# Building a Toeplitz bias matrix by two DMAs through a skewed DRAM scratch instead of a Hankel load and matmuls with a flipped identity

## The chip, the cores and the metric

The kernel runs on one core of a Trainium2 chip. The metric is the device time of one execution in microseconds (us): the median of three runs is 929.63 us (929.59 to 930.97). All data is float32; TensorE multiplies it in split form, as a high part plus a low part.

## What is computed

One layer of a hybrid encoder runs for two groups that share the weights: a prompt of 512 tokens and a sample of 32 new tokens with a cache of 512 keys and values. So there are T = 544 token columns, a model width of 1024, 8 attention heads of 64 and 4 retention heads of 128. What the change touches is the relative-position bias of the attention:

```python
def chunk_attention_prompt(q, k, v, table):          # table: (8, 257)
    ...
    dist = jnp.arange(CHUNK)[:, None] - r[None, :] + ATT_WINDOW
    bias = table[:, jnp.clip(dist, -REL_CLIP, REL_CLIP) + REL_CLIP].astype(jnp.float32)
    ...
    s = jnp.where(valid[None, :, None, None, :], s + bias[None, None], -jnp.inf)
    p = jax.nn.softmax(s, axis=-1).astype(v.dtype)

z   = rms_norm(x) @ w_in                             # 1024 x 5632, all branches
mix = (sigmoid(ga) * (A @ w_attn_out) + sigmoid(gb) * (R @ w_ret_out)) @ w_o
x   = x + rms_norm(mix)
x   = x + rms_norm(relu(rms_norm(x) @ w_ff_up)^2 @ w_ff_down)
```

The bias of a query and a key depends on their distance alone, so for each head it is a Toeplitz matrix: constant along its diagonals. Beyond a distance of 128 it is one value, and a constant added to a whole row falls out of the softmax, so the kernel stores bias minus this far value, for 128 queries by 256 nearest keys and 8 heads: a tile of 128 x 8 x 256, 1 MB.

## The kernel before

Activations lie transposed (features on partitions, 544 tokens along the row). Every projection is cut into column tiles of 128 outputs, grouped by four; "group g, tile j" is column_tile(g, j). A tile is 96 matmul instructions of 272 columns: 8 slices of the contraction, 2 halves of the tokens, and the three products high x high, high x low and low x high. Weights stream in by SyncE's DMA queue, half a megabyte per transfer, into w_raw, which has two halves (buffers) for two tiles each. For each tile ScalarE makes the high part w_hi (split_hi, L493), VectorE the low part w_lo (split_lo, L1116), and TensorE waits for the low part (L776) before the tile. VectorE takes each finished tile from PSUM to z (to_z, L1126).

The order on each engine is written out by hand, and engines meet by semaphores:

- SyncE loads x (five transfers), the first 128 columns of w_in (w_first), the next 128 columns, the cached keys k_cache (1 MB, L363), then the second buffer of w_raw in two transfers (L351, L352). Later loads wait until a buffer's low parts are made.
- TensorE transposes x, runs tiles (0,0) and (0,1), waits for k_cache and transposes it, then runs tiles (0,2) and (0,3) and groups 1 and 2. Tile (0,2) needs both transfers of the second buffer, through L493 and L1116.
- GpSimd prepares the bias table at the start (L396 to L405). It loads the 8 x 257 table, fills each row up to 384 with its last value, stores the 8 rows of 1536 B in DRAM (table_ext, 12 KB), waits until that has landed, and loads a Hankel matrix from it: partition p of head h gets 256 values from place 1 + p on. The rows overlap in DRAM; the load moves 1 MB.
- After group 2 TensorE waits for the Hankel tile and turns it into the Toeplitz form: 16 calls (8 heads by 2 blocks of 128) of a matmul with the flipped identity, which the profile shows as 32 matmuls (L856). They go to the PSUM tile wk. VectorE then subtracts the far value (L1186, from PSUM and hankel into bias), masks a block (L1189) and raises bias_ready.
- The attention loop follows, one pass for two heads. TensorE runs tile (3,0), then waits for pair_ready, bias_ready and attT_ready (L918 to L920) and transposes keys and values. VectorE, behind the bias, copies k_pair and v_pair (L1112), makes low parts, takes tile (3,0) and copies the transposed keys to k_nat (L1254, L1255). TensorE runs tile (3,1) and waits for k_nat before the scores.

ScalarE issues the DMAs of the identity, the gains, the ones and the flipped identity (L501 to L504) ahead of its first work. GpSimd has nothing else to do until the attention ends.

Of the kernel before, what the change touches and what calls it, by code (L numbers as in the profile page):

```python
# [1 line left out]

# [4 lines left out]
D = 1024  # L35
P = 128
KT = D // P
SEQ, DEC = 512, 32
T = SEQ + DEC
# [3 lines left out]
AH, AD = 8, 64  # L43
# [4 lines left out]
TABLE = 2 * CLIP + 1  # L48
# [6 lines left out]
Z_AQ, Z_AK, Z_AV, Z_GATE, Z_SPARE, Z_RQ, Z_RK, Z_RV, Z_RG, Z_SLOTS = 0, 4, 8, 4, 12, 20, 24, 28, 32, 36  # L55


def shape_constants():

    f = np.float32  # L60
    ident = np.eye(P, dtype=f)
    flip = np.ascontiguousarray(ident[::-1])
    half = RD // 2
    inv = (f(10000.0) ** (-np.arange(half, dtype=f) / f(half))).astype(f)
    pos = np.concatenate([np.arange(SEQ), PAST + np.arange(DEC)]).astype(f)
    ang = (inv[:, None] * pos[None, :]).astype(f)
    cos = np.cos(ang.astype(np.float64)).astype(f)
    sin = np.sin(ang.astype(np.float64)).astype(f)
    rope = np.zeros((P, 2, T), f)
    rope[:half, 0] = rope[half:, 0] = cos  # L70

    rope[half:, 1] = -sin
    rope[:half, 1] = sin
    decay = np.zeros((P, RH, RC), f)
    t = np.arange(P)
    for h in range(RH):
        lg = np.log1p(-np.exp2(-5.0 - h))

        key = RD ** -0.5
        decay[:, h, :P] = np.where(t[None, :] >= t[:, None], key * np.exp(-(t[:, None] + 1.0) * lg), 0.0)  # L80
        decay[:, h, P] = np.exp((t + 1.0) * lg)
        decay[:, h, P + 1] = key * np.exp((P - 1.0 - t) * lg)
        decay[:DEC, h, P + 2] = key * np.exp((DEC - 1.0 - t[:DEC]) * lg)
        decay[:, h, P + 3] = np.exp(P * lg)
        decay[:, h, P + 4] = np.exp(DEC * lg)
    return {"ident": ident, "flip": flip, "ones": np.ones((P, P), f), "rope": rope, "decay": decay}


class Order:
# [23 lines left out]
def build(nc, a, outs):  # L113
    fp, fr = mybir.dt.float32, mybir.dt.float32r
    ALU, ACT, AX = mybir.AluOpType, mybir.ActivationFunctionType, mybir.AxisListType
    ctx = ExitStack()

    with ctx:
        def sem(name):
            return ctx.enter_context(nc.semaphore(name))  # L120
# [7 lines left out]
        def place(name, shape, dtype=fp, at=None):  # L128

            size = 4 * int(np.prod(shape[1:]))  # L130
            size += -size % 32
            where = top[0] if at is None else at
            if at is None:
                top[0] += size
                assert top[0] <= first + arena_bytes, (name, top[0] - first - arena_bytes)
            ends[name] = where + size
            return nc.alloc_sbuf_tensor_at(name, shape, dtype, offset=where)

        ends = {}
# [8 lines left out]
        ident = place("ident_sb", [P, P])  # L148
        ones = place("ones_sb", [P, P])
# [4 lines left out]
        rope = place("rope_sb", [P, 2, T])  # L154
        decay = place("decay_sb", [P, RH, RC])
# [8 lines left out]
        z_at = top[0]  # L164
# [9 lines left out]
        y_out = place("y_out", [P, 5, D], at=z_at + 4 * T * Z_RQ)  # L174

        x_nat = place("x_nat", [P, 5, D], at=z_at)
        hankel = place("hankel", [P, AH, 2 * P], at=z_at + 4 * T * Z_RQ)
        k_cache = place("k_cache", [P, 4, AH * AD], at=ends["hankel"])
        table_row = place("table_row", [AH, 3 * P], at=ends["k_cache"])
        flip = place("flip_sb", [P, P], at=ends["table_row"])  # L180
        x_waste = place("x_waste", [P, 2, D], at=ends["flip_sb"])
        assert ends["x_nat"] <= z_at + 4 * T * Z_SPARE and ends["x_waste"] <= work_at

        bias = place("bias", [P, AH, 2 * P], at=z_at + 4 * T * Z_SPARE)
# [50 lines left out]
        wk = ctx.enter_context(nc.psum_tensor("wk", [P, 2048], fp))  # L235
        wk_halves = [wk[:, 1024 * i:1024 * i + 1024].rearrange("p (n c) -> p n c", n=2) for i in range(2)]

        table_ext = nc.dram_tensor("table_ext", (AH, 3 * P), fp, kind="Internal").ap()


        ident_in, const_in = sem("ident_in"), sem("const_in")
        x_in = [sem(f"x_in{t}") for t in range(5)]
        w_first, w_in_sem = sem("w_first"), [sem("w_loaded0"), sem("w_loaded1")]
        cache_k_in, table_in, table_filled, table_out, hankel_in = (
            sem("cache_k_in"), sem("table_in"), sem("table_filled"), sem("table_out"), sem("hankel_in"))
        gains_in, x_tr, x_copied_act, x_copied_dve = sem("gains_in"), sem("x_tr"), sem("x_copied_act"), sem("x_copied_dve")
        x_hi, x_lo, x_sum_act, var_clear = sem("x_hi"), sem("x_lo"), sem("x_sum_act"), sem("var_clear")
        kc_tr, kc_ready, bias_mm, bias_ready = sem("kc_tr"), sem("kc_ready"), sem("bias_mm"), sem("bias_ready")
        sum_mm, var_ready, std_ready, tok_rstd_ready, spread_mm, rstd_ready = (
            sem("sum_mm"), sem("var_ready"), sem("std_ready"), sem("tok_rstd_ready"), sem("spread_mm"), sem("rstd_ready"))  # L250
        hi_ready, lo_ready, mm_done, acc_free = sem("hi_ready"), sem("lo_ready"), sem("mm_done"), sem("acc_free")
# [37 lines left out]
        def halves(ap):  # L289
            return ap.rearrange("p (n c) -> p n c", n=2)  # L290
# [103 lines left out]
        def _(pool):  # L394
            order = Order(pool, pool_order)
            pool.dma_start(table_row[:, 0:TABLE], a["rel_bias_table"]).then_inc(table_in, 16)  # L396

            pool.wait_ge(table_in, 16)
            pool.tensor_copy(table_row[:, TABLE:3 * P],
                             table_row[:, TABLE - 1:TABLE].to_broadcast([AH, 3 * P - TABLE])).then_inc(table_filled, 1)  # L400
            pool.wait_ge(table_filled, 1)
            pool.dma_start(table_ext, table_row[:]).then_inc(table_out, 16)

            pool.wait_ge(table_out, 16)
            pool.dma_start(hankel[:], bass.AP(table_ext.tensor, 1, [[1, P], [3 * P, AH], [1, 2 * P]])).then_inc(hankel_in, 16)  # L405

            pool.wait_ge(scores_mm, 2 * PAIRS)
            pool.dma_start(rope[:], a["rope"]).then_inc(ret_const_in, 16)  # L408
# [79 lines left out]
        def _(act):  # L488
# [12 lines left out]
            act.dma_start(ident[:], a["ident"]).then_inc(ident_in, 16)  # L501
            act.dma_start(gains[:], a["gains"]).then_inc(gains_in, 16)
            act.dma_start(ones[:], a["ones"]).then_inc(const_in, 16)
            act.dma_start(flip[:], a["flip"]).then_inc(const_in, 16)  # L504
            for counter, n in CREDITS.items():
                act.sem_inc(counter, n)
            act.preload_act_table(ACT.Sqrt)
# [252 lines left out]
        def _(pe):  # L760
            def products(dst, whi, wlo, k, hi, lo, start, stop):

                for w, h, begin, end in ((whi, hi, start, False), (whi, lo, False, False), (wlo, hi, False, stop)):
                    for n in range(2):
                        ins = pe.matmul(dst[:, n, 0:HALF], w[:, k, :], h[:, k, HALF * n:HALF * n + HALF], start=begin, stop=end)  # L765
                return ins
# [20 lines left out]
            def tr(out, in_):  # L787
                n = in_.shape[0]
                return pe.transpose(out, in_, ident[0:n, 0:n])  # L789
# [3 lines left out]
            for t, (s, n) in enumerate(TILES):  # L793
# [5 lines left out]
                for k in range(KT):  # L799
                    ins = tr(ps[:, k, :], x_nat[0:n, t, P * k:P * k + P])  # L800
# [37 lines left out]
            for p in range(PAIRS):  # L838
                for t in range(4):
                    ins = tr(wk[:, 512 * p + P * t:512 * p + P * t + P], k_cache[:, t, P * p:P * p + P])  # L840
# [6 lines left out]

            pe.wait_ge(hankel_in, 16)  # L850
            pe.wait_ge(const_in, 32)

            pe.wait_ge(kc_ready, 1)
            for h in range(AH):
                for b in range(2):
                    ins = pe.matmul(wk[:, 256 * h + P * b:256 * h + P * b + P], hankel[:, h, P * (1 - b):P * (1 - b) + P], flip[:],  # L856
                                    start=True, stop=True)
            ins.then_inc(bias_mm, 1)


            def scores(i, e):
# [52 lines left out]
            with pe.Fori(0, PAIRS) as i:  # L914
# [35 lines left out]
                for t, (s, n) in enumerate(TILES):  # L950
                    ins = tr(wk[:, s:s + n], att_nat[0:n, t, :])
# [3 lines left out]
            with pe.Fori(0, RH) as i:  # L955
# [16 lines left out]
                for t, (s, n) in enumerate(TILES):  # L972
                    ins = pe.matmul(wk[:, 1024 + RD * t:1024 + RD * t + RD], rk_nat[0:n, t, :], rv_nat[0:n, t, :], start=True, stop=True)  # L973
# [4 lines left out]
                for t, (s, n) in enumerate(TILES):  # L978
                    out = wk[0:n, RD * t:RD * t + RD]
                    alone = t == 0  # L980
                    ins = pe.matmul(out, ret_a[0:n, s:s + n], rv_nat[0:n, t, :], start=True, stop=alone)  # L981
                    if t == 4:
                        ins = pe.matmul(out, rq[:, s:s + n], state_in[:, bass.ds(i, 1), :].rearrange("p a c -> p (a c)"), start=False, stop=True)
                    elif t:
                        ins = pe.matmul(out, rq[:, s:s + n], states[:, t - 1, :], start=False, stop=True)
                ins.then_inc(ret_o_mm, 1)
                column_tile(g, 3, act_hi, act_lo, half_used=h_half_used)
                for t, (s, n) in enumerate(TILES):
# [3 lines left out]
                    ins = tr(wk[:, 1024 + s:1024 + s + n], ret_n[0:n, t, :])  # L992
# [23 lines left out]
            for k in range(KT):  # L1016
                pe.wait_ge(h2_lo, k + 1)
                for j in range(2):
# [3 lines left out]
                    ins = products(acc[j], w_hi[:, j], w_lo[:, j], k, act_hi, act_lo, k == 0, k == KT - 1)  # L1022
# [4 lines left out]
            for k in range(KT):  # L1027
                if k == 3:
                    spread(2)
                ins = products(wk_halves[1], w_hi_third, w_lo_third, k, act_hi, act_lo, k == 0, k == KT - 1)  # L1030
# [32 lines left out]
            for part, (s, n) in enumerate(PARTS):  # L1063
                for j in range(2):
                    if part == 0:
                        pe.wait_ge(lo_ready, 4 * (G_FFN + 15) + 3 + j)
                    for k in range(KT):
# [7 lines left out]
                        ins = pe.matmul(dst, w_lo[:, j, k, :], mid_hi[:, k, s:s + n], start=False, stop=(k == KT - 1))  # L1075
# [31 lines left out]
        def _(dve):  # L1107
            order = Order(dve, dve_order)
# [71 lines left out]
            with dve.Fori(0, G_RET) as g:  # L1180
                for j in range(4):
                    to_z(g, j, 4 * g + j)
                    split_ahead(g, j)

            dve.wait_ge(bias_mm, 1)
            order.after(dve.tensor_tensor(bias[:], wk[:].rearrange("p (h c) -> p h c", h=AH),  # L1186
                                          hankel[:, :, 2 * P - 1:2 * P].to_broadcast([P, AH, 2 * P]), ALU.subtract))

            dve.memset(bias[0:AD, :, P + AD:2 * P], NEG).then_inc(bias_ready, 1)  # L1189
            order.flatten()  # L1190
# [172 lines left out]
            with dve.Fori(0, 2) as i:  # L1363
                for j in range(4):
# [5 lines left out]
                    ins = dve.tensor_tensor(halves(part_b[:]), wk_halves[j % 2][:, :, 0:HALF],  # L1370
                                            z[:, bass.ds(Z_GATE + KT + m, 1), :].rearrange("p a (n c) -> p (a n) c", n=2), ALU.mult)
# [163 lines left out]
```

## Time and profile before

| | us |
|---|---|
| median of three runs | 929.63 (929.59 to 930.97) |
| span of the profiled execution | 929.0 |
| TensorE matmul busy | 886.9 (95%) |
| TensorE weight load busy | 867.7 (93%) |
| VectorE busy | 476.3 (51%) |
| ScalarE busy | 315.9 (34%) |
| GpSimd busy | 99.0 (11%) |

The profile is one execution: all its times start at the first instruction, and durations are those of this execution. The trace has a chain of waits (the work that ended last, followed back), a timeline for each engine, sums by stretch of time with TensorE's granted clock and the share of time in which the 16 DMA engines were busy, and for the DMA queues the packets, the megabytes and the share of the 16 engines' time that these packets took. That share can be over 100%, where packets overlap. Queue q1 is SyncE's, q10 ScalarE's and q0 GpSimd's.

### The profile page before, as it was taken

Reading aid. Unit: us, or ns where it says so; the run is one execution under the profiler, and the core shown is the slowest. Engines: PE = TensorE matmul, PEld = TensorE weight load, DVE = VectorE, ACT = ScalarE, POOL = GpSimd, SP = SyncE. Lnnn points to the kernel's source line nnn. Section 1 sums busy time; section 2 is a strip of 40 time slices with the busy share of each in tenths; the row PEclk is TensorE's granted clock in tenths of the full one; section 3 lists DMA queues with packets and bytes.
Section 4 is the critical chain, followed back from the end, with each engine's and each line's share of the span. In section 5 each row is a group of like instructions: output and inputs, shape, how many; then the busy total and the mean of one; then the engine's idle time right before and its main releaser. Section 6 shows DMA issues by size and latency. Waiting matters only on the chain.

```text
span 929.0 us, 17032 instructions
## 1 busy us (share of the span) xinstructions
PE 886.9 (95%) x6908; PEld 867.7 (93%) x6908; DVE 476.3 (51%) x735; ACT 315.9 (34%) x457; POOL 99.0 (11%) x71
## 2 busy tenths in 40 slices
PE   7999999999988989899998799999999999999997
PEld 6999999999977978889997699999999999999996
DVE  6233766666758467476534844334433443344326
ACT  6212544445323132245423333113311332133322
POOL 1000000000123031120221700000000000000132
PEclk9999999999988989999998799999999999999997
DMA  9323232122321112112222022222222222222202
GB/s 294 101 78 99 70 102 69 56 69 80 112 78 45 51 45 96 51 46 91 90 91 90 1 83 91 73 80 88 88 91 90 90 90 90 90 92 90 91 1 96
DMA packets 78449, 77.18 MB, mean 83 GB/s; under 512 B 2944, under 2 KB 76304, under 8 KB 78416
## 3 DMA queue, kind: packets, MB, share of 16 engines
q1 hardware_dynamic: 69328, 70.53, 23.1%
q10 hardware_dynamic: 8448, 4.02, 1.6%
q0 software_dynamic: 640, 2.17, 0.7%
q8 instruction: 24, 0.39, 0.2%
q14 instruction: 9, 0.07, 0.0%
HBM read 71.70 MB, written 4.99 MB: 83 GB/s over the span
## 4 chain that ended last, share of the span: by engine, by line
PE 89%; DVE 7%; issue 2%; ACT 1%; POOL 1%; DMA 0%; DVEq 0%; ACTq 0%
PE acc L765 73%; PE wk L789 4%; PE wk L765 3%; PE wk L903 3%; DVE rope_k L1292 2%; DVE scaled L1399 1%; DVE act_lo L1419 1%; PE wk L865 1%; PE wk L864 1%; DVE rk L1293 1%; POOL act_lo L433 1%; PE wk L973 1%; PE wk L822 1%; PE acc L789 1%; PE wk L981 1%
## 5 line engine op out<-in xcount | busy, mean ns | idle before, releaser
L493 ACT ACTIVATE w_hi<-w_raw 128x1024 fp32r<-128x1024 f32 x123 | 130.4, 1060 | 469.3 <-PE acc L765 455.2
L765 PE MATMUL acc<-act_hi,w_hi 128*128 128x272 f32 x1264 | 270.8, 296 | 11.8 <-DVE act_lo L1419 8.6
L765 PE MATMUL acc<-act_hi,w_lo 128*128 128x272 f32 x1264 | 265.2, 292 | 0.0
L765 PE MATMUL acc<-act_lo,w_hi 128*128 128x272 f32 x1264 | 264.6, 291 | 0.0
L765 PEld LDWEIGHTS acc<-act_hi,w_hi 128*128 128x128 f32 x1264 | 202.6, 192 | 17.6 <-DVE act_lo L1419 9.8
L765 PEld LDWEIGHTS acc<-act_lo,w_hi 128*128 128x128 f32 x1264 | 202.5, 192 | 0.0
L765 PEld LDWEIGHTS acc<-act_hi,w_lo 128*128 128x128 f32 x1264 | 201.2, 192 | 0.0
L1116 DVE TENSOR_TENSOR w_lo<-w_raw,w_hi 128x1024 fp32r<-128x1024 f32 x123 | 150.3, 1222 | 35.0 <-ACT w_hi L493 34.9
L765 PE MATMUL acc<-mid_hi,w_hi 128*128 128x272 f32 x608 | 125.4, 287 | 0.0
L765 PE MATMUL acc<-mid_hi,w_lo 128*128 128x272 f32 x608 | 125.0, 288 | 0.0
L765 PE MATMUL acc<-mid_lo,w_hi 128*128 128x272 f32 x608 | 124.8, 287 | 0.0
L765 PEld LDWEIGHTS acc<-mid_lo,w_hi 128*128 128x128 f32 x608 | 95.0, 188 | 0.0
L765 PEld LDWEIGHTS acc<-mid_hi,w_lo 128*128 128x128 f32 x608 | 94.7, 188 | 0.0
L765 PEld LDWEIGHTS acc<-mid_hi,w_hi 128*128 128x128 f32 x608 | 94.7, 188 | 0.0
L1126 DVE TENSOR_TENSOR z<-acc,rstd 128x544 f32 (+1 forms) x44 | 31.8, 722 | 97.9 <-PE acc L765 97.6
L1458 DVE TENSOR_TENSOR y_ffn<-y_ffn,acc 128x544 f32 (+1 forms) x30 | 21.6, 721 | 107.9 <-PE acc L765 107.9
L439 POOL TENSOR_TENSOR sqsum<-sqsum,sq 128x544 f32<-128x544 f32 x20 | 34.4, 1720 | 379.5 <-ACT sq L728 353.4
L1436 DVE SCALAR_TENSOR_TENSOR relu<-acc,rstd 128x544 f32<-128x544 f32 x31 | 22.4, 724 | 81.5 <-PE acc L765 81.4
L562 ACT ACTIVATE probs<-wk,neg_max 128x512 f32<-128x512 f32 (+4 forms) x40 | 22.2, 558 | 16.9 <-DVE neg_max L1215 16.8
L1441 DVE TENSOR_TENSOR mid_lo<-relu,mid_hi 128x544 f32 (+1 forms) x32 | 23.2, 725 | 7.6 <-ACT mid_hi L706 7.5
L408 POOL DMA_DIRECT2D rope_sb<-in_rope x1 | 0.6, 550 | 224.8 <-PE wk L865 224.8
L424 POOL TENSOR_TENSOR rope_q<-rq,rope_sb 64x544 f32<-64x544 f32 x8 | 12.3, 1537 | 93.7 <-DVE rq L1112 93.3
(206 smaller groups left out, 881.6 us busy)
## 6 DMA issues: line engine op xcount, KB each, us to landing
w_raw<-in_w_in SPq DMA_DIRECT2D x44, 512.0 KB, 4.3
w_raw<-in_w_ff_up SPq DMA_DIRECT2D x32, 512.0 KB, 4.3
w_raw<-in_w_ff_down SPq DMA_DIRECT2D x32, 512.0 KB, 4.1
w_raw<-in_w_o SPq DMA_DIRECT2D x8, 512.0 KB, 3.9
x_nat<-in_x_prompt SPq DMA_DIRECT2D x4, 512.0 KB, 5.2
w_raw<-in_w_attn_out SPq DMA_DIRECT2D x4, 512.0 KB, 3.5
w_raw<-in_w_ret_out SPq DMA_DIRECT2D x4, 512.0 KB, 4.5
k_cache<-in_cache_attn_k SPq DMA_DIRECT2D x1, 1024.0 KB, 11.8
```

Source lines behind the costliest of these rows:

```text
L439: pool.tensor_tensor(sqsum[:], sqsum[:], sq[:, m % 2, :], ALU.add).then_inc(sq_added, 1)
L493: act.activation(w_hi[:, v % 2], w_raw[:, v // 2, :, P * (v % 2):P * (v % 2) + P], ACT.Copy).then_inc(hi_ready, 1)
L562: act.activation(probs[0:n, P_COL[t]:P_COL[t] + WIDTH[t]], wk[0:n, S_COL[t]:S_COL[t] + WIDTH[t]], ACT.Exp, bias=neg_max[0:n, t:t + 1], acc ...
L765: ins = pe.matmul(dst[:, n, 0:HALF], w[:, k, :], h[:, k, HALF * n:HALF * n + HALF], start=begin, stop=end)
L789: return pe.transpose(out, in_, ident[0:n, 0:n])
L903: ins = pe.matmul(out, probsT[:, PT_COL[t] + n * b:PT_COL[t] + n * b + n], v, start=(b == 0), stop=(t < 4 and b == blocks - 1))
L1116: dve.tensor_tensor(w_lo[:, v % 2], w_raw[:, v // 2, :, P * (v % 2):P * (v % 2) + P], w_hi[:, v % 2].bitcast(fp), ALU.subtract).then_inc(l ...
L1126: dve.tensor_tensor(z[:, bass.ds(slot, 1), :].rearrange("p a (n c) -> p (a n) c", n=2), acc[j % 2][:, :, 0:HALF], halves(rstd[:]), ALU.mul ...
L1292: dve.tensor_tensor(rope_k[to:to + RD // 2, :], row(Z_RK + i, frm, frm + RD // 2), rope[frm:frm + RD // 2, 1, :], ALU.mult)
L1436: dve.scalar_tensor_tensor(halves(relu[:, j % 2, :]), src[:, :, 0:HALF], 0.0, halves(rstd[:]), ALU.max, ALU.mult).then_inc(acc_free, 1)
L1441: dve.tensor_tensor(mid_lo[:, bass.ds(4 * i + j, 1), :].rearrange("p a c -> p (a c)"), relu2[:, j % 2, :], mid_hi[:, bass.ds(4 * i + j, 1) ...
L1458: dve.tensor_tensor(y, y, acc[j % 2][:, :, 0:HALF], ALU.add).then_inc(acc_free, 1)
```

## The change

The scratch in DRAM becomes an array of 8 heads x 128 rows, with a row pitch of 385 elements. GpSimd fills a second tile, table_back, with each head's 384 values in reverse order: 127 copies of the last value, then the 257 table values backwards. One DMA writes every head's row 128 times, each copy into its own row of the scratch; this is 1.57 MB, in 1024 rows of 1536 B, whose source is eight SBUF partitions. A second DMA reads with a step of 384 from the start of one row to the next, one less than the pitch, so that row p starts p values earlier: that is the Toeplitz form, and it goes straight into bias. The 16 matmul calls, TensorE's wait for them, the Hankel tile, the flipped identity and its load fall away. VectorE waits for the DMA instead of for TensorE, copies the far value of each head to a small tile and subtracts it in place.

```diff
-        hankel = place("hankel", [P, AH, 2 * P], at=z_at + 4 * T * Z_RQ)
+        table_row = place("table_row", [AH, 3 * P], at=z_at + 4 * T * Z_RQ)
+        table_back = place("table_back", [AH, 3 * P], at=ends["table_row"])
+        bias_far = place("bias_far", [P, AH], at=ends["table_back"])
...
-        table_ext = nc.dram_tensor("table_ext", (AH, 3 * P), fp, kind="Internal").ap()
+        SKEW = 3 * P + 1
+        table_skewed = nc.dram_tensor("table_skewed", (AH, P, SKEW), fp, kind="Internal").ap()
+        table_ext = table_skewed[:, :, 0:3 * P]
...
-            pool.tensor_copy(table_row[:, TABLE:3 * P],
-                             table_row[:, TABLE - 1:TABLE].to_broadcast([AH, 3 * P - TABLE])).then_inc(table_filled, 1)
+            pool.tensor_copy(table_back[:, 0:3 * P - TABLE], table_row[:, TABLE - 1:TABLE].to_broadcast([AH, 3 * P - TABLE]))
+            pool.tensor_copy(table_back[:, 3 * P - TABLE:3 * P], table_row[:, 0:TABLE][:, ::-1]).then_inc(table_filled, 1)
             pool.wait_ge(table_filled, 1)
-            pool.dma_start(table_ext, table_row[:]).then_inc(table_out, 16)
+            pool.dma_start(table_ext, table_back[:].unsqueeze(1).to_broadcast([AH, P, 3 * P])).then_inc(table_out, 16)

             pool.wait_ge(table_out, 16)
-            pool.dma_start(hankel[:], bass.AP(table_ext.tensor, 1, [[1, P], [3 * P, AH], [1, 2 * P]])).then_inc(hankel_in, 16)
+            pool.dma_start(bias[:], bass.AP(table_ext.tensor, P - 1, [[3 * P, P], [P * SKEW, AH], [1, 2 * P]])).then_inc(hankel_in, 16)
...
-            act.dma_start(flip[:], a["flip"]).then_inc(const_in, 16)
...
-            pe.wait_ge(hankel_in, 16)
-            pe.wait_ge(const_in, 32)
+            pe.wait_ge(const_in, 16)

             pe.wait_ge(kc_ready, 1)
-            for h in range(AH):
-                for b in range(2):
-                    ins = pe.matmul(wk[:, 256 * h + P * b:256 * h + P * b + P], hankel[:, h, P * (1 - b):P * (1 - b) + P], flip[:],
-                                    start=True, stop=True)
-            ins.then_inc(bias_mm, 1)
...
-            dve.wait_ge(bias_mm, 1)
-            order.after(dve.tensor_tensor(bias[:], wk[:].rearrange("p (h c) -> p h c", h=AH),
-                                          hankel[:, :, 2 * P - 1:2 * P].to_broadcast([P, AH, 2 * P]), ALU.subtract))
+            dve.wait_ge(hankel_in, 16)
+            order.after(dve.tensor_copy(bias_far[:], bias[:, :, 0]))
+            order.after(dve.tensor_tensor(bias[:], bias[:], bias_far[:].unsqueeze(2).to_broadcast([P, AH, 2 * P]), ALU.subtract))
```

## Rows read from the trace of the kernel before

**Rows 1.** Sums by stretch: from:to, length, busy of PE PEld DVE ACT POOL, PEclk, DMA.

```profile
30.00:89.00 59.00, 59.00 (x473) 59.00 (x473) 17.56 (x18) 10.84 (x10) 0.00 (x0) 1.00 0.27 89
97.00:245.00 148.00, 148.00 (x1208) 141.59 (x1206) 99.21 (x209) 76.61 (x149) 1.83 (x3) 1.00 0.25 78
```

**Rows 2.** Chain of waits, 0 to 125 us: start, length, what.

```profile
27.63 1.75 PE wk L789 x16
29.37 60.14 PE acc L765 x480
89.52 3.57 PE wk L856 x32
93.09 6.02 PE acc L765 x48
99.11 1.09 PE wk L789 x10
```

**Rows 3.** VectorE's timeline, 84 to 112 us: start, length, instruction [idle before <-releaser].

```profile
90.64 1.23 DVE L1116 TENSOR_TENSOR w_lo<-w_raw,w_hi 128x1024 fp32r<-128x1024 f32 x1 [0.26 <-ACT w_hi L493]
93.12 2.29 DVE L1186 TENSOR_TENSOR bias<-wk,hankel 128x2048 f32<-128x2048 f32 x1 [1.26 <-PE wk L856]
95.58 0.48 DVE L1189 MEMSET bias<- 64x512 f32 x1 [0.17 <-DVE bias L1186]
96.29 0.42 DVE L1112 TENSOR_SCALAR v_pair<-z 128x544 f32 x1
...
103.54 0.27 DVE L1255 COPY k_nat<-wk 32x128 f32<-32x128 f32 x1
```

**Rows 4.** Timeline of all engines at the start of the execution.

```profile
6.37 0.28 POOL L399 COPY table_row<-table_row 8x127 f32<-8x127 f32 x1 [4.38 <-DMA table_row<-in_rel_bias_table]
6.95 0.54 POOL L402 DMA_DIRECT2D table_ext<-table_row  x1 [0.30 <-POOL table_row L399]
...
10.53 0.83 SPq L352 DMA_DIRECT2D w_raw<-in_w_in  x1
...
11.27 0.17 DVE L1149 TENSOR_SCALAR tok_var<-tok_var 128x5 f32<-128x5 f32 x1
...
13.23 0.94 POOL L405 DMA_DIRECT2D hankel<-table_ext  x1 [5.75 <-DMA table_ext<-table_row]
...
21.64 1.06 ACT L493 ACTIVATE w_hi<-w_raw 128x1024 fp32r<-128x1024 f32 x1 [2.33 <-PE acc L765]
...
22.82 1.21 DVE L1116 TENSOR_TENSOR w_lo<-w_raw,w_hi 128x1024 fp32r<-128x1024 f32 x1
```

**Rows 5.** DMA issues: KB, us to landing (w_raw: that issued at 10.53).

```profile
w_raw<-in_w_in SPq DMA_DIRECT2D x1, 512.0 KB, 10.9
...
hankel<-table_ext POOLq DMA_DIRECT2D x1, 1024.0 KB, 8.8
```

**Rows 6.** DMA queues, 12.2 to 21.5 us: packets, MB, share of 16 engines.

```profile
q1 hardware_dynamic: 1806, 2.20, 71.3%
q0 software_dynamic: 277, 1.05, 33.2%
```

**Rows 7.** DMA queues, 18 to 21 us, the Hankel load beside w_raw.

```profile
q0 software_dynamic: 226, 0.93, 90.3%
q1 hardware_dynamic: 136, 0.12, 14.1%
```

**Rows 8.** DMA queues, 13 to 15 us, k_cache, in rows of 2 KB.

```profile
q1 hardware_dynamic: 374, 0.77, 103.5%
```

**Rows 9.** DMA queues, 7.5 to 8.0 us, x_nat on 128 partitions.

```profile
q1 hardware_dynamic: 42, 0.17, 83.6%
```

**Rows 10.** DMA queues, 927.8 to 928.1 us, y_sample's store from 32 partitions.

```profile
q1 hardware_dynamic: 18, 0.07, 88.7%
```

**Rows 11.** Sums by stretch, in the retention: columns as in rows 1.

```profile
255.00:259.50 4.50, 1.39 (x12) 1.17 (x10) 4.44 (x4) 2.98 (x3) 4.34 (x3) 1.00 0.50 175
259.50:266.30 6.80, 5.47 (x25) 5.34 (x26) 4.39 (x7) 2.04 (x4) 2.54 (x2) 0.50 0.00 0
```

More of the change, by code:

```diff
@@ L61, in shape_constants @@
     ident = np.eye(P, dtype=f)
-    flip = np.ascontiguousarray(ident[::-1])
     half = RD // 2
@@ L85, in shape_constants @@
         decay[:, h, P + 4] = np.exp(DEC * lg)
-    return {"ident": ident, "flip": flip, "ones": np.ones((P, P), f), "rope": rope, "decay": decay}
+    return {"ident": ident, "ones": np.ones((P, P), f), "rope": rope, "decay": decay}
 class Order:
@@ L176, in build @@
         x_nat = place("x_nat", [P, 5, D], at=z_at)
-        hankel = place("hankel", [P, AH, 2 * P], at=z_at + 4 * T * Z_RQ)
[L178 to L181, printed above, removed]
+        table_row = place("table_row", [AH, 3 * P], at=z_at + 4 * T * Z_RQ)
+        table_back = place("table_back", [AH, 3 * P], at=ends["table_row"])
+        bias_far = place("bias_far", [P, AH], at=ends["table_back"])
+        k_cache = place("k_cache", [P, 4, AH * AD], at=ends["bias_far"])
+        x_waste = place("x_waste", [P, 2, D], at=ends["k_cache"])
         assert ends["x_nat"] <= z_at + 4 * T * Z_SPARE and ends["x_waste"] <= work_at
@@ L247, in build @@
         x_hi, x_lo, x_sum_act, var_clear = sem("x_hi"), sem("x_lo"), sem("x_sum_act"), sem("var_clear")
-        kc_tr, kc_ready, bias_mm, bias_ready = sem("kc_tr"), sem("kc_ready"), sem("bias_mm"), sem("bias_ready")
+        kc_tr, kc_ready, bias_ready = sem("kc_tr"), sem("kc_ready"), sem("bias_ready")
         sum_mm, var_ready, std_ready, tok_rstd_ready, spread_mm, rstd_ready = (
```

## The prediction

> **What bounds the kernel now.** I read the sums by stretch first: which engine is full where the change acts? TensorE is busy for all of 30 to 89 us and of 97 to 245 us [rows 1]. The chain of waits says the same, and gives the price of what falls away: from 27.63 us to the attention the chain is TensorE alone, piece behind piece, and the 32 matmuls stand in it with 3.57 us [rows 2]. So the first question is how much of 3.57 us survives. The second is what the first 30 us can bear, for the change puts a new transfer of 1.57 MB there. For that I read the timeline of the start, then the DMA queues in narrow stretches.
>
> **What falls away on TensorE.** The 32 matmuls last 3.57 us, and nothing else would fill this time: tile (3,0) starts at 89.52 instead of 93.09, and TensorE wants the transposed keys at 99.11 - 3.57 = 95.54 [rows 2]. There it waits for v_pair and the bias, which VectorE makes. Before, VectorE idled 1.26 us for TensorE ahead of the subtraction at 93.12, and v_pair ended at 96.29 + 0.42 = 96.71 [rows 3]: it had 2.4 us in hand. After, VectorE can go on when w_lo ends, at 90.64 + 1.23 = 91.87 [rows 3]. It adds the copy of 8 far values. The trace has no such copy; the nearest row is the 5-column operation of 0.17 us [rows 4], and behind it the hand-over that stands between subtraction and mask, 0.17 us [rows 3]. The subtraction can start at 92.2, 0.9 us earlier than before. Its operand comes from SBUF instead of PSUM: the same 2048 elements at the rate of the low parts (1024 in 1.23 us, from SBUF) would be 2.46 us instead of 2.29 [rows 3], so from 0 to 0.2 us more; I take 0. Then v_pair ends at about 95.8, and TensorE waits some 0.3 us (0.2 to 0.6). Its next meeting with VectorE: k_nat was ready 7.1 us after v_pair (103.54 + 0.27 - 96.71) [rows 3], and TensorE comes there 1.09 + 6.02 = 7.11 us after its wait [rows 2]. That is a tie, worth 0 to 0.1 us. Gain: 3.57 - 0.3 = 3.3 us, bounds 2.8 and 3.6. What comes later in the attention follows TensorE, and 97 to 245 us is full [rows 1], so it passes the gain on. The dropped load of the flipped identity ends no wait and is worth nothing.
>
> **What is added on GpSimd.** The reversed copy has twice the columns of the copy of 0.28 us [rows 4], so up to 0.56 us more; the write is then issued at 7.0 to 7.5 instead of 6.95. GpSimd has nothing queued behind it that anyone needs before 245 us. The Hankel load, issued at 13.23, moved 0.93 of its 1.05 MB after 18.0 [rows 4, 6, 7]: data flows some 4.8 us after an issue. The write's data therefore starts at about 12.3. The read back is 1 MB in rows of 1 KB as the Hankel load was, which landed in 8.8 us [rows 5]. VectorE needs it only at 91.9. Even with a write of 30 us it lands at about 52, and 40 us of TensorE work cover it.
>
> **How long the write takes.** 1024 rows of 1536 B, read from eight partitions. No row has this form, so I bound it. The free end: k_cache's 2 KB packets took 103.5% x 16 x 2 / 374 = 0.089 us each [rows 8]. If eight DMA engines take a head each, 128 rows at no more than that are 11.3 us; on sixteen, 5.7 us. The slow end: with 128 partitions, a packet of 4 KB took 83.6% x 16 x 0.5 / 42 = 0.159 us [rows 9]. In the store of y_sample, from 32 partitions, the 16 packets that make up its 0.07 MB took 88.7% x 16 x 0.3 / 16 = 0.266 us [rows 10]. So 32 partitions give 16 x 4096 B / 0.266 us = 246 GB/s. If the limit goes with the partitions touched, eight give 62 GB/s, and 1.573 MB take 25.6 us. I take the slow end: the partition rows are nearest in kind, since they show a store slowed by few partitions alone. In the Trainium skill, "SBUF — State Buffer", section "Door 1: The DMA port swizzle", partitions 0 to 3 share one port with a measured 27.6 GB/s; by that rule partitions 0 to 7 reach two ports and the write would last some 28 us, an estimate by that page. The trace agrees in direction: 32 partitions were slowed, 128 not [rows 9, 10].
>
> **Who stands behind the write.** From 12.2 us on, SyncE's queue has 1806 packets left for w_in, k_cache and the second buffer of w_raw, 113 for each DMA engine [rows 6]. The last load was issued at 10.53 and landed at 21.4, and ScalarE used it at 21.64 [rows 4, 5]. From there to the end of w_lo at 22.82 + 1.21 = 24.03 are 2.4 us, and TensorE wants tile (0,2) at 29.37 [rows 2, 4]: 5.3 us in hand. Beside the Hankel load, this queue got 136 packets to 226 of q0 and 14% of the time to 90% [rows 7]. Its packets are 0.9 KB, those of q0 4.1 KB: they take turns by packet, not by time. With such turns, a write whose packets last long starves the loads on the DMA engines they share. The 4.1 KB packets hold four source rows of 1 KB each, so I take two rows of 1536 B for a packet of the write: 64 turns on each of eight DMA engines in 25.6 us. At 12.3 + 25.6 = 37.9 us the loads have had 64 of 113 turns; the other 49 at 71.3% x 16 x 9.3 / 1806 = 0.059 us [rows 6] take 2.9 us. The second buffer lands at 40.8, w_lo ends at 43.2, and TensorE stalls 43.2 - 29.4 = 13.8 us. With single rows for packets there are 128 turns, the 113th at 34.9, and the stall is 8 us. With sixteen DMA engines (32 turns each), it is 43.2 + 1.9 - 29.4 = 15.7 us. With 28 to 30 us of write it is up to 18 us. k_cache is ahead of w_raw in the same queue and is late too, but tile (0,2) waits for the later, so its delay lies inside.
>
> **The clock.** After a stretch in which TensorE was busy 1.39 of 4.5 us, the granted clock stood at 0.50, its lower level of 1.2 GHz, for 6.8 us [rows 11]. A stall of 14 us idles it more. At most 6.8 us at half speed are lost, 3.4 us, at least none if the clock is back before the stall ends; I take 1.7.
>
> **The sum**, against the median, which lies 0.6 us above the profiled span: 929.6 - 3.3 + 13.8 + 1.7 = 941.8 us. Its own range is 929.6 - 3.6 + 8 = 934 to 929.6 - 2.8 + 18 + 3.4 = 948.
>
> **Rivals.** First, the start bears it (chance 0.28): the write runs near the free end on sixteen DMA engines, or the loads pass it by. Sixteen engines need 5.7 us for it where the Hankel load had 33.2% x 9.3 = 3.1 [rows 6]: the last load lands 2.6 us later, inside the 5.3 us. Then the gain stands: 929.6 - 3.3 = 926.3 us, 925.8 to 927. For it speaks that the loads have slack; against it, the partition rows. Second, the write is free but sits on eight DMA engines (0.10): 11.3 us of write and 113 x 0.059 = 6.7 us of loads end at 30.3, w_lo at 32.7, the stall is 3.3 us, and it eats the gain: 929.6 us. Third, the scratch is so slow that VectorE waits (0.04): it decides once write and read together land past 91.9 instead of about 52, and needs a write of over 65 us, less than 24 GB/s. Nothing in the trace is so slow; it would come on top of a stall in the loads, 965 us or more. The forecast case has 0.58. A rule against it would be that DMA engines let other queues pass a slow packet. In the Trainium skill, "DMA: Bandwidth & Descriptors", section "Queues, rings and completion order", an engine takes the queues in turn and drains a whole packet before it switches. That agrees with rows 7; whether a slow reading side holds the turn, no row here shows.
>
> **Range and chances.** From 925.9 to 947.5: it reaches from the first rival through the second to nearly all of the forecast case. A measurement of this kernel can tell 0.2% (1.9 us) from no change. Slower by more than that: forecast case and third rival, 0.61 with a little taken off for a stall just over 3.3 us. Within 0.2%: 0.11. Faster: 0.28.
>
> **What would show it.** The write: its time from issue to landing in the DMA issues (30 us here, under 17 if free), and the megabytes of q0 by stretch from 12 us on. The starving: the last w_raw load issued near 10.5 landing near 41, packets of q1 few beside q0. The stall: TensorE idle before tile (0,2), released through L1116 and L493, and a granted clock of 0.5 behind it. The gain: no matmuls between groups 2 and 3, and a wait of about 0.3 us for v_pair. If the last w_raw load lands before 26.5 us, the forecast is wrong at the write's length or at the turns, and the first rival holds.

## The result and the profile after

The changed kernel takes 947.96 us (median of five runs, 946.70 to 948.47) against 929.65 us (five runs). The ratio estimated from the runs is 1.018, 95% interval 1.016 to 1.019; the two medians alone give 1.020, a little above it. It is slower, as forecast; the time lies half a microsecond above the upper end of my range. Medians of the kernel before differ by up to 3 us between the sets of runs below, so kernels are compared by such a ratio within a set, given below with its 95% interval.

The chain of waits of the changed kernel, from 4 to 120 us (start, length, what), against rows 2:

```profile
4.31 6.69 SPq L336
...
11.04 4.73 SPq L324
...
15.81 31.15 DMA w_raw<-in_w_in
...
47.04 1.06 ACT w_hi L466
...
48.13 1.24 DVE w_lo L1082
...
49.41 61.59 PE acc L737 x480
111.00 0.02 issue
...
117.10 1.31 PE wk L761 x10
```

Where rows 2 have TensorE from 27.63 us on, there is now a DMA of w_raw of 31.15 us. Tile (0,2) starts at 49.41 instead of 29.37 us: +20.04. The ten tiles to the end of group 2 take 61.59 instead of 60.14: +1.45. From there to the transposes of keys and values it is 117.10 - 111.00 = 6.10 instead of 99.11 - 89.52 = 9.59: -3.49. The sum is +18.0; the spans differ by 946.7 - 929.0 = 17.7.

The DMA issues of the same run (KB, us to landing), where rows 5 had 8.8 for the Hankel load:

```profile
table_skewed<-table_back POOLq DMA_DIRECT2D x1, 1536.0 KB, 35.9
k_cache<-in_cache_attn_k SPq DMA_DIRECT2D x1, 1024.0 KB, 39.8
bias<-table_skewed POOLq DMA_DIRECT2D x1, 1024.0 KB, 8.8
```

The write lasts 35.9 us from its issue at 7.49. The k_cache load, in whose way it stands, takes 39.8. The read back takes 8.8, lands near 52.5 and is wanted at 113. Now the DMA queues in two stretches, 14 to 20 us and 30 to 40 us (packets, MB, share of 16 engines), which answer to rows 7:

```profile
q0 software_dynamic: 64, 0.29, 49.7%
q1 hardware_dynamic: 460, 0.65, 31.5%
...
q0 software_dynamic: 100, 0.46, 44.6%
q1 hardware_dynamic: 101, 0.21, 5.3%
```

In the second stretch q0 and q1 move a packet each in turn, 100 to 101. A packet of q0 is 4.6 KB, three rows of the scratch, and holds a DMA engine for 44.6% x 16 x 10 / 100 = 0.71 us. One of q1, a k_cache row of 2 KB, takes 0.08 us. So q1 moves 21 GB/s, where it had 385 in rows 8. The sum of the shares is 50%. That fits one half of the DMA engines full and the other half, which have done their part of the loads, idle; the views don't show single engines.

The sums by stretch show the clock (columns as in rows 1):

```profile
27.00:43.00 16.00, 1.73 (x14) 1.51 (x13) 0.00 (x0) 0.00 (x0) 0.00 (x0) 0.65 0.52 74
43.00:49.40 6.40, 3.68 (x16) 3.28 (x16) 1.27 (x2) 2.36 (x3) 0.93 (x1) 0.50 1.01 342
49.40:56.20 6.80, 6.79 (x44) 6.79 (x44) 1.72 (x2) 1.41 (x1) 0.00 (x0) 0.78 0.69 227
56.20:111.00 54.80, 54.80 (x441) 54.80 (x440) 17.55 (x18) 9.55 (x9) 0.00 (x0) 1.00 0.24 77
```

TensorE idles and is granted 0.50, the lower level of 1.2 GHz. It is still 0.50 when tile (0,2) starts and comes back some 3 us later (the mean of 0.78 over 6.8 us is 3.0 us at 0.50); half of that is the 1.45 us.

### The profile page after: what moved, and what is told of

It is laid out like the page before. It is cut to its first block, busy times and chain, and to the rows that moved or that the text cites. A ratio compares the mean times of both kernels' runs of the same rounds, so it can differ in the third digit from the quotient of the medians.

```text
span 946.7 us, 16969 instructions
## 1 busy us (share of the span) xinstructions
PE 885.2 (94%) x6876; PEld 866.0 (91%) x6876; DVE 476.3 (50%) x736; ACT 315.5 (33%) x457; POOL 99.9 (11%) x72
## 4 chain that ended last, share of the span: by engine, by line
PE 84%; DVE 7%; DMA 3%; issue 2%; SPq 2%; ACT 1%; POOL 1%; DVEq 0%; ACTq 0%
PE acc L737 69%; PE wk L737 3%; DMA w_raw<-in_w_in 3%; PE wk L761 3%; PE wk L869 2%; DVE rope_k L1258 2%; DVE scaled L1365 1%; DVE act_lo L1385 1%; PE wk L830 1%; PE wk L831 1%; DVE rk L1259 1%; SPq L336 1%; POOL act_lo L406 1%; PE wk L939 1%; PE wk L794 1%
## 5 line engine op out<-in xcount | busy, mean ns | idle before, releaser
L678 ACT ACTIVATE mid_hi<-relu 128x544 f32 (+1 forms) x32 | 21.1, 659 | 3.4
## 6 DMA issues: line engine op xcount, KB each, us to landing
table_skewed<-table_back POOLq DMA_DIRECT2D x1, 1536.0 KB, 35.9
```

The lines of the kernel that those rows point to most:

```text
L678: act.activation(mid_hi[:, 4 * i + j, :], relu2[:, j % 2, :], ACT.Copy).then_inc(f_hi, 1)
```

## The experiments

My theory: the write reads eight neighbouring partitions, is slow for that, and starves the loads by taking turns with them, packet by packet, on the DMA engines they share. The rivals: rows at odd places in DRAM make the write slow; it is the number of source partitions and not where they are; the loss is in the new bias wait or in VectorE's order; only the crowded start is the matter.

**The write alone.**

```diff
+            pool.dma_start(table_skewed[:, :, 0:3 * P], table_row[:].unsqueeze(1).to_broadcast([AH, P, 3 * P])).then_inc(skew_out, 16)
             pool.dma_start(table_ext, table_row[:]).then_inc(table_out, 16)
```

> The kernel before, with the large write alone added: 1.57 MB of copies of the eight table rows into a second scratch that nobody reads, issued just ahead of the 12 KB write; the Hankel load and the 32 matmuls stay. If the write is the whole loss: tile (0,2) starts near 49.4 us instead of 29.4, the lower clock costs some 1.5 us, and as nothing is gained the time is 929.6 + 20.0 + 1.5 = 951 us (948 to 953). If the loss lies elsewhere in the change (the bias wait, the new VectorE order), the time stays at 930.

Ratio 1.0205 (1.0172 to 1.0238), 951.76 us against 932.24. The write in its DMA issues (KB, us to landing):

```profile
table_skewed<-table_row POOLq DMA_DIRECT2D x1, 1536.0 KB, 35.9
```

Its chain of waits (start, length, what):

```profile
48.96 60.40 PE acc L769 x480
109.36 3.57 PE wk L860 x32
112.93 6.02 PE acc L769 x48
```

The same write, nearly the same stall (48.96 - 29.37 = 19.6 us), with the 32 matmuls still in place. The write is the whole loss; the rest of the change is only gain. The clock is another matter: the ten tiles took 60.40 us, 0.26 more than before, where I expected 1.5. The granted clock was back at 1.00 from 47.4 us on, behind the transposes of k_cache and before tile (0,2).

**Aligned rows.** The same eight partitions, a pitch of 2048 B in the scratch.

```diff
-        SKEW = 3 * P + 1
+        SKEW = 4 * P
...
-            pool.dma_start(bias[:], bass.AP(table_ext.tensor, P - 1, [[3 * P, P], [P * SKEW, AH], [1, 2 * P]])).then_inc(hankel_in, 16)
+            pool.dma_start(bias[:], bass.AP(table_ext.tensor, P - 1, [[SKEW - 1, P], [P * SKEW, AH], [1, 2 * P]])).then_inc(hankel_in, 16)
```

> The changed kernel with a row pitch of 2048 B instead of 1540 B in the scratch, so that every row starts aligned. If the write is slow because its source is eight partitions: unchanged, the write lands about 36 us after its issue, stall 20 us, 947 us. If it is slow because rows start at odd places in DRAM: a packet of 4.6 KB takes some 0.18 us instead of 0.74, the write lands in 12 us or less, the stall is under 3 us and the time 926 to 930 us.

Ratio 1.0158 (1.0128 to 1.0187), 947.38 us; the write lands in 35.8 us and tile (0,2) starts at 49.17. Whether the rows start aligned in DRAM has no part in it.

**Eight partitions, elsewhere.** The heads on partitions 0, 4 ... 28. The two table tiles become 32 partitions high, and GpSimd clears table_row ahead of the load; the write is issued at 7.54 us instead of 7.49.

```diff
-            pool.dma_start(table_row[:, 0:TABLE], a["rel_bias_table"]).then_inc(table_in, 16)
+            pool.dma_start(table_row[0:4 * AH:4, 0:TABLE], a["rel_bias_table"]).then_inc(table_in, 16)
...
-            pool.dma_start(table_ext, table_back[:].unsqueeze(1).to_broadcast([AH, P, 3 * P])).then_inc(table_out, 16)
+            pool.dma_start(table_ext, table_back[0:4 * AH:4, :].unsqueeze(1).to_broadcast([AH, P, 3 * P])).then_inc(table_out, 16)
```

> The changed kernel with the eight table rows on partitions 0, 4, 8 ... 28 instead of 0 to 7; number of source partitions, packets and DMA engines as before. If the rate goes with the number of partitions touched (as the prediction took it): unchanged, 947 us. If neighbouring partitions share a way out of SBUF and these eight don't: a packet takes 0.18 to 0.2 us, the write 43 x 0.25 = 11 us, the loads are through at 12.3 + 43 x 0.18 + 113 x 0.06 = 27 us, tile (0,2) is late by 0 to 1 us, and the time is 926 to 928 us.

Ratio 0.9950 (0.9912 to 0.9988), 927.05 us: from 18 us slower to faster than the kernel before, by a step of 4 in a partition index. The write lands in 16.6 us, and still runs on eight DMA engines: from 20 to 22 us q0 has 34.7% of the sixteen and q1 16.1%, half in all. Its DMA queues from 16 to 22 us (packets, MB, share of 16 engines):

```profile
q1 hardware_dynamic: 669, 0.86, 38.8%
q0 software_dynamic: 184, 0.85, 34.9%
```

A packet takes 34.9% x 16 x 6 / 184 = 0.18 us instead of 0.75 (49.7% x 16 x 6 / 64, above). VectorE's timeline has the low part that tile (0,2) needs:

```profile
27.72 1.22 DVE L1085 TENSOR_TENSOR w_lo<-w_raw,w_hi 128x1024 fp32r<-128x1024 f32 x1 [4.48 <-ACT w_hi L469]
```

It is ready at 28.94, and TensorE comes to tile (0,2) at 29.69, behind its own work: no stall, with 0.75 us to spare. The number of partitions, packets and bytes is unchanged, so the rule I used in the prediction, a rate that goes with the number of partitions, is wrong.

**The step between.** The heads on partitions 0, 2 ... 14; the diff is against the kernel with 0, 4 ... 28.

```diff
-            pool.dma_start(table_row[0:4 * AH:4, 0:TABLE], a["rel_bias_table"]).then_inc(table_in, 16)
+            pool.dma_start(table_row[0:2 * AH:2, 0:TABLE], a["rel_bias_table"]).then_inc(table_in, 16)
...
-            pool.dma_start(table_ext, table_back[0:4 * AH:4, :].unsqueeze(1).to_broadcast([AH, P, 3 * P])).then_inc(table_out, 16)
+            pool.dma_start(table_ext, table_back[0:2 * AH:2, :].unsqueeze(1).to_broadcast([AH, P, 3 * P])).then_inc(table_out, 16)
```

> The changed kernel with the eight table rows on partitions 0, 2, 4 ... 14, halfway between 0 to 7 (packets of 4.6 KB in 0.74 us, stall 20 us) and 0, 4 ... 28 (0.18 us, no stall). If four neighbouring partitions share one way out of SBUF, two heads now share one: a packet takes 0.36 us, the write 43 x 0.36 = 15.6 us from 12.2 to 28 us, the loads have 70 turns left at 0.054 us and land near 31.6, tile (0,2) starts near 34, stall 4.7 us, time 929.6 - 3.5 + 4.7 + (0 to 1.7 for the clock) = 931 to 932.5 us. If only direct neighbours get in each other's way: 0.18 us a packet and 926 to 928 us.

Ratio 1.0018 (1.0006 to 1.0031), 933.13 us against 931.20. DMA queue q0 from 16 to 22 us:

```profile
q0 software_dynamic: 120, 0.55, 40.3%
```

The chain of waits:

```profile
34.27 62.87 PE acc L740 x480
```

A packet takes 40.3% x 16 x 6 / 120 = 0.32 us, and the stall is 34.27 - 29.37 = 4.9 us (4.7 expected). With one, two and four heads in each group of four neighbouring partitions, a packet takes 0.18, 0.32 and 0.75 us. Four at once are 4 x 4.6 KB / 0.75 us = 25 GB/s for such a group, two are 29 GB/s. One head alone gets 25 too, and there I take the DMA engine for the limit: in rows 9 a packet of 4 KB took 0.159 us, 26 GB/s, in a load to 128 partitions. That is argued and not tested. The clock cost 62.87 - 60.14 = 2.7 us.

In the Trainium skill, "SBUF — State Buffer", section "Door 1: The DMA port swizzle", partitions 0 to 3 share one port and 4 to 7 another, and a transfer on 0 to 3 measured 27.6 GB/s. The three placements agree with that: 25 and 29 GB/s where a group is shared, and no such loss where each head has a group to itself.

**Half the write**, from partitions 0 to 7: 64 rows a head, two reads of every second partition. (An earlier form, the changed kernel with 64 of the 128 copies left out, gave no time.)

```diff
-        SKEW = 3 * P + 1
+        ROWS, STEP = 64, 2
+        SKEW = 3 * P + STEP
...
+            for q in range(STEP):
+                pool.dma_start(bias[q:P:STEP], bass.AP(table_ext.tensor, P - 1 - q, [[3 * P, ROWS], [ROWS * SKEW, AH], [1, 2 * P]])).then_inc(hankel_in, 16)
```

> The changed kernel with 64 rows a head in the scratch (pitch 386 elements) and two reads of every second partition, so half the write from the same eight partitions 0 to 7. If long packets take turns with the loads: 22 turns at 0.74 us, the write ends near 28 us, the loads have 113 - 22 = 91 turns left at 0.054 us and land near 33, tile (0,2) starts near 35.4, stall 6 us, time 932 to 934 us. If half the write costs half the stall: 10 us, 937 us.

Ratio 1.0029 (1.0016 to 1.0043), 934.68 us against 931.20. The chain:

```profile
15.40 17.59 DMA w_raw<-in_w_in
...
35.44 63.11 PE acc L739 x480
```

The stall is 35.44 - 29.37 = 6.1 us (6 expected), under a third of the full one for half the write. That is what the turns give: the 5.3 us in hand are used up first, and the turns left over when the write ends run fast. The ten tiles took 63.11 us, so the clock cost 3.0 us here, more than behind the stall of 20 us: the granted clock was 0.50 from 35.4 to 41.3 us.

**Spread over all partitions.** Sixteen copies of each head's row on 128 partitions, the same bytes to the same places in DRAM.

```diff
+            for h in range(AH):
+                pool.dma_start(table_row[16 * h:16 * h + 16, 0:TABLE], a["rel_bias_table"][h:h + 1, :].to_broadcast([16, TABLE])).then_inc(table_in, 16)
...
+            pool.dma_start(table_skewed.rearrange("h (r q) s -> (h r) q s", q=8)[:, :, 0:3 * P],
+                           table_back[:].unsqueeze(1).to_broadcast([P, 8, 3 * P])).then_inc(table_out, 16)
```

> The changed kernel with the table on all 128 partitions (16 copies of each head's row, brought there by eight small loads); each partition writes 8 rows. The 1.57 MB in DRAM are the same bytes at the same places. If the eight source partitions are the cause: packets of 4.6 KB take some 0.18 us on sixteen DMA engines, the write lands within 10 us of its issue, the loads are late by 3 us at most and inside their slack, the stall of tile (0,2) is gone, and the whole of the gain shows: 929.6 - 3.5 = 926.1 us (925.7 to 927.5). If any write of 1.57 MB at the start starves the loads: 935 us or more.

Ratio 0.9975 (0.9964 to 0.9986), 928.96 us against 931.01. The DMA queues from 18 to 21 us:

```profile
q0 software_dynamic: 144, 0.66, 91.1%
q1 hardware_dynamic: 139, 0.14, 16.1%
```

The chain of waits:

```profile
16.00 14.14 PE acc L739 x96
30.14 1.75 PE wk L763 x16
31.89 3.13 PE acc L739 x25
```

VectorE's timeline, the low part for tile (0,2):

```profile
28.50 1.23 DVE L1084 TENSOR_TENSOR w_lo<-w_raw,w_hi 128x1024 fp32r<-128x1024 f32 x1 [3.49 <-ACT w_hi L468]
```

No load is waited for at tile (0,2): TensorE goes from 30.14 to 31.89 to 35 without a gap. The turns are still one to one, and a packet takes 91.1% x 16 x 3 / 144 = 0.30 us, on all sixteen DMA engines at once. I expected 0.18; why it is longer is open. Two things make this experiment weaker than it looks. The eight small loads of the table delay the write's issue to 12.61 us, 5 us later than in the changed kernel, so more of the loads were through before it. And the slack was all but gone: the low part was ready at 29.73, in time only because TensorE came at 31.89 instead of 29.37. The time of the profiled execution, 930.42 us, the slowest of the set's twelve, is above my 926 us in part because tiles (0,0) and (0,1) took 14.14 us, where the last kernel below takes 12.26. TensorE had a granted clock of 0.51 from 13.2 to 20.1 us in this execution, which is the lower level. The cause of this early fall is open. The set's twelve times lie between 927.0 and 930.4, and no trace shows whether the clock is what parts them.

**A later write.** GpSimd waits for the second buffer of w_raw first.

```diff
+            pool.wait_ge(w_in_sem[1], 32)
             pool.dma_start(table_ext, table_back[:].unsqueeze(1).to_broadcast([AH, P, 3 * P])).then_inc(table_out, 16)
```

> The changed kernel with GpSimd waiting for the second buffer of w_raw (landed at 21.4 us in the kernel before) ahead of the large write, so that no load of the start stands beside it. Data flows from about 26 to 57 us. If only the crowded start is the matter, the stall is gone and the time is 926 us. If turns with long packets starve whatever load runs beside them: the load of group 1's second buffer, issued near 30 us, needs 64 turns a DMA engine and gets some 35 until the write ends, lands near 59 us, while TensorE wants its tile near 53.5; stall 5 to 10 us, time 931 to 937 us.

Ratio 1.0160 (1.0136 to 1.0183), 946.30 us, outside what either theory gave. The timelines of GpSimd and SyncE:

```profile
19.46 1.12 POOL L376 DMA_DIRECT2D table_skewed<-table_back  x1 [12.27 <-DMA w_raw<-in_w_in]
...
21.49 4.52 SPq L325 DMA_DIRECT2D w_raw<-in_w_in  x1
```

The chain of waits:

```profile
21.49 34.59 DMA w_raw<-in_w_in
...
58.53 50.79 PE acc L738 x384
```

I had the write's data start 4.8 us after its issue, as rows 4, 6 and 7 show for the full queues of the start. Here the queues are emptier, and q0 has 26% of the DMA time from 20 to 22 us. So the write is ahead of the next two loads of w_raw, issued at 20.92 and 21.49, and not behind them. Together they need 64 turns on each DMA engine and get no more than the write's 43 in the write's 33 us; the second lands 34.6 us after its issue. TensorE, done with tile (0,3) at 40.9, waits 17.6 us for tile (1,0). The mechanism holds, and the start is not special: this write also starved the 1 MB for the next two tiles.

**A small write.** 16 rows a head, eight reads (ROWS, STEP = 16, 8 in the diff of half the write).

> The changed kernel with a scratch of 16 rows a head instead of 128 (pitch 392 elements), written in one DMA of 0.2 MB from the same eight partitions, and eight reads of 16 partitions each, every eighth partition. The write is 6 packets for each of eight DMA engines at 0.74 us, 4.5 us. The loads lose some 4 us, inside the 5.3 us of slack; the eight reads move 1 MB before 40 us and are needed at 89. By the theory: stall 0 to 1 us, 926 to 927.5 us. If the number of DMAs on GpSimd's queue or reads from few partitions matter: 930 us or more.

Ratio 0.9958 (0.9942 to 0.9974), 927.63 us against 931.01. The write lands in 7.0 us. But the last load of w_raw landed at 12.50 + 14.85 = 27.35: the eight reads now stand beside it, with 237 packets of q0 to 258 of q1 from 18 to 22 us. Tile (0,2) started at 29.80, after TensorE had waited 0.40 us for its low part: the slack was used up to the end.

**Small, spread and later.** As that, with the heads on partitions 0, 4 ... 28, and the reads behind the last load of w_raw, which landed near 20 us:

```diff
             pool.wait_ge(table_out, 16)
+            pool.wait_ge(w_in_sem[1], 32)
```

> The changed kernel with 16 rows a head in the scratch, the heads on partitions 0, 4 ... 28, and the eight reads held back until the second buffer of w_raw has landed, so that nothing large stands beside the loads of the start. By the theory the last w_raw load lands near 21.5 us, tile (0,2) starts at 29.4 as before, and the whole gain of 3.5 us shows: 926.1 us (925.5 to 927).

Ratio 0.9959 (0.9945 to 0.9972), 927.37 us against 931.20 in its set, a gain of 3.8 us. Its chain of waits:

```profile
15.21 12.26 PE acc L743 x96
...
29.21 60.14 PE acc L743 x480
...
95.45 1.31 PE wk L767 x10
96.76 6.02 PE acc L743 x48
```

VectorE's timeline:

```profile
91.61 0.17 DVE L1158 COPY bias_far<-bias 128x8 f32<-128x8 f32 x1
91.81 2.29 DVE L1159 TENSOR_TENSOR bias<-bias,bias_far 128x2048 f32<-128x2048 f32 x1
...
94.97 0.42 DVE L1084 TENSOR_SCALAR v_pair<-z 128x544 f32 x1
```

Tile (0,2) starts at 29.21, no clock is lost, and 29.21 + 60.14 to 95.45 is 6.10 us, the same 3.49 us less than before as in the changed kernel. This is what the idea is worth with its loss taken out. Its interval overlaps those of the kernel before it and of the heads on 0, 4 ... 28 with the full write, so these runs don't rank the three.

## Why the prediction was right, and where its sizes were off

The forecast of +12.2 us (13.8 + 1.7 - 3.3) became +18.0 in the trace. The mechanism was the forecast one; the term that was mis-sized is the stall, by 6.2 us, and of these the length of the write is 5.3.

**The gain: right.** Forecast 3.57 - 0.3 = 3.3 us, measured 3.49. The wait for v_pair was 0.08 us instead of 0.3. The copy of the far values took the 0.17 us of its row but started before w_lo had ended (113.26 against 113.35), and the subtraction took 2.29 us from SBUF as from PSUM (113.46 and 91.81, as in rows 3). The transposes of keys and values behind it took 1.31 us, where rows 2 have 1.09; I did not foresee that, and its cause is open.

**The start of the write: right.** Issued at 7.49, its data flows from 12.2 us on.

**The length of the write: mis-sized, and its rule wrong.** I took 246 GB/s of 32 partitions down to 62 GB/s for eight, so 25.6 us. It was 31 us, from 12.2 to 43.2, or 51 GB/s. These are two faults. The rule was wrong: what rows 10 showed was not 32 partitions but eight groups of four, and the eight heads had two groups; eight partitions with a group each cost nothing that shows. But for partitions 0 to 7 both rules give the same, since 8 of 32 partitions are also 2 of 8 groups. It is luck of this placement that the wrong rule did no harm. The size came from the rate in rows 10: 0.3 us of a store, 31 GB/s a group, where the write had 25. The estimate that I gave beside the Trainium skill's rule, 28 us, was nearer, and its rule was the right one.

**The turns: right in kind, mis-sized.** Turns are one to one (100 to 101). But a packet holds three rows, not two, so the write gives the loads 43 turns and not 64: of 113, 70 were left when it ended, where I had 49. That fits k_cache, whose last packet is the 49th turn (the other 64 are w_raw's): it landed at 44.1, just behind the write. The last load landed at 15.81 + 31.15 = 46.96, 3.8 us after the write, where I had 2.9. In the Trainium skill, "DMA: Bandwidth & Descriptors", section "Why a DMA increments its semaphore by 16 and not by 1", a DMA runs on the largest number of engines up to sixteen that divides the outermost dimensions of both its sides. The shares agree: 44.6% of sixteen is seven to eight engines for eight heads.

**The stall: 13.8 forecast, 20.0 measured.** The write's end is 5.3 us later than forecast (43.2 against 37.9), the rest of the turns another 0.9. The w_hi and w_lo behind it took 49.41 - 46.96 = 2.45 us, as forecast. The upper end of my range for the stall, 18 us, went with 30 us of write but with 64 turns; it did not join the slow ends of both terms. Its own range ended at 948 us, and the stated one at 947.5; this is why the range ended just below the result.

**The clock: near, by luck.** 1.7 forecast, 1.45 measured. But the write alone and the aligned pitch, with stalls as long, lost 0.3 us, and the stalls of 5 and 6 us lost 2.7 and 3.0. What the clock cost did not follow the length of the stall; my bounds of 0 and 3.4 held in all of them.

**The cover of the read back and of k_cache: right.** The read back landed 60 us ahead of its use; k_cache landed at 44.1 us and its delay lay inside that of w_raw.

**The rivals.** Neither free write occurred in the changed kernel. The kernel with the heads on 0, 4 ... 28 is the second rival as I described it, a fast write on eight DMA engines, and I had its price wrong. I gave it a stall of 3.3 us and no gain. It had no stall and the whole gain, since I had put all 113 turns of the loads behind the write, against my own rule of turns: 43 of them ran beside it, and the low part was ready at 28.94 where I had 32.7. The spread source comes nearest to the first rival, sixteen DMA engines, with packets that were slower than I had them and a later start. The slow scratch, the third, did not occur: the read back landed 60 us before its use. Nor did it matter how the rows lie in DRAM: the aligned pitch changed nothing.

## What to carry to other kernels

A transfer nobody waits for still has a price: count, on each DMA engine, how many packets of others stand beside it, how long one of its packets holds the engine, and which load behind it has the least slack. A DMA that reads a few rows many times over should have its sources spread over SBUF: a step of four partitions took away a stall of 20 us here. Cost the stretch of time in which the transfer runs separately from the rest of the kernel: here the loads of the start had 5.3 us of slack, and a write issued 12 us later starved the next loads instead.

## What the runs showed of the hardware that I had not expected

- A packet from SBUF took 0.18, 0.32 or 0.75 us by whether one, two or four of eight source partitions lay in a group of four neighbours.
- Three rows of 1536 B went in one packet of 4.6 KB in every kernel that wrote the scratch in full. Ahead of them q0 had a burst of small packets: from 12 to 13 us in the changed kernel 376 packets with 0.11 MB. What these carry the trace does not say.
- In the kernel with the spread source a packet took 0.30 us, though 128 partitions were read.
- SyncE stood in the issue of a load while earlier loads of its queue were unfinished: one issue of w_raw took 20.02 us in the changed kernel, where others take 0.4. It delayed nothing further, since what stood behind it was needed later still. The last load for tile (0,2) was itself issued at 15.81 instead of 10.53, behind longer issues; k_cache, ahead of it in the queue, landed only at 44.1, so this did not set its landing.

The timeline of SyncE in the changed kernel:

```profile
15.81 4.54 SPq L325 DMA_DIRECT2D w_raw<-in_w_in  x1
21.08 20.02 SPq L324 DMA_DIRECT2D w_raw<-in_w_in  x1
41.28 1.02 SPq L325 DMA_DIRECT2D w_raw<-in_w_in  x1
51.29 0.37 SPq L324 DMA_DIRECT2D w_raw<-in_w_in  x1
```

- The first packets of a DMA issued by GpSimd flowed some 4.7 us after the issue beside full queues (changed kernel: 7.49 to 12.2) and within 2 us beside emptier ones (later write: issued at 19.46, 71 packets from 21.0 to 21.5).
- In the profiled executions of four kernels (the changed one, the write alone, the aligned pitch, the spread source) TensorE's clock fell to 0.5 for some microseconds between 12 and 20 us; in that of the kernel before it did not. It cost 1.9 us in the spread kernel; in the other three TensorE waits for the loads afterwards anyway. Its cause was not sought.
